# Sixteen small matmuls and a bias row replaced, and convolution taps, weight splits and a square root reordered, in the mixer of a two-block transformer kernel

## The reference, cut to what matters

```
h = layer_norm(x, ln_in_g, ln_in_b)
for l in range(DEPTH):
    proj = h @ w_in[l]
    a_in, b_q, b_k, b_v, c_in, d_cq, d_ckv, d_kr = split(proj)
    a = a_in[..., :256] * sigmoid(a_in[..., 256:])
    a = depthwise_conv(a, conv_a_w[l], conv_a_b[l])          # 31 taps
    o_a = silu(layer_norm(a, ln_a_g[l], ln_a_b[l]))
    o_b = attention(rope(rms(b_q)), rope(rms(b_k)), b_v)     # 4 heads, 2 kv heads
    c = gelu(c_in); u, sv = c[..., :256], c[..., 256:]
    sv = layer_norm(sv, sgu_ln_g[l], sgu_ln_b[l])            # in 4 groups of 64 channels
    sv = einsum('gpq,bnqgc->bnpgc', sgu_w[l], sv) + sgu_b[l].T[:, :, None]
    o_c = u * sv
    o_d = latent_attention(d_cq, d_ckv, d_kr)                # 4 heads, low rank q and k/v
    mix = concatenate([o_a, o_b, o_c, o_d]) @ w_out[l]
    h = layer_norm(ALPHA * h + mix, ...)
    ... feed-forward with a 3-tap convolution, layer_norm
```

## Time and profile before

| | us |
|---|---|
| median of 3 runs | 1983.23 |
| lowest and highest of them | 1982.24, 1985.15 |
| profiled execution, its own time | 1978.52 |
| profiled execution, span of its instructions | 1976.7 |
| PE busy in the span | 1858.6 (94%) |
| DVE busy | 1257.8 (64%) |
| ACT busy | 903.0 (46%) |
| mean granted clock of TensorE | 0.968 |

### The profile page before, as it was taken

One profiled execution on the slowest core, in us unless ns is written; L12 is line 12 of the kernel. 1 busy time (PEld: TensorE's weight loads), 2 busy tenths in 40 slices (PEclk: granted clock), 3 DMA queues, 4 the chain that ended last, 5 costly groups with the idle time before them and its releaser, 6 DMA issues.

```text
span 1976.7 us, 31350 instructions
## 1 busy us (share of the span) xinstructions
PE 1858.6 (94%) x12558; PEld 1683.4 (85%) x12571; DVE 1257.8 (64%) x1550; ACT 903.0 (46%) x1088; POOL 110.2 (6%) x79
## 2 busy tenths in 40 slices
PE   7997699999759999999999999999999998899999
PEld 7975599988549998899898888999899987789998
DVE  5775786787568777655666655555555566546555
ACT  5553454445335444433454555333433357545332
POOL 0300110011002000000016000000000000000000
PEclk9997899999779999999999999999999998999999
DMA  8531265543216554555453362555555542335553
GB/s 296 183 128 52 77 213 191 183 144 113 85 43 222 179 179 145 192 191 181 141 157 120 139 223 87 195 187 191 166 190 186 191 151 86 124 103 166 181 190 127
DMA packets 227044, 311.34 MB, mean 157 GB/s; under 512 B 6615, under 2 KB 199415, under 8 KB 226327
## 3 DMA queue, kind: packets, MB, share of 16 engines
q1 hardware_dynamic: 224038, 298.07, 45.2%
q0 software_dynamic: 2640, 10.66, 1.7%
q10 hardware_dynamic: 288, 1.54, 0.2%
HBM read 307.09 MB, written 3.15 MB: 157 GB/s over the span
## 4 chain that ended last, share of the span: by engine, by line
PE 87%; DVE 5%; ACT 5%; issue 2%; DMA 0%; DVEq 0%; ACTq 0%
PE bank L691 46%; PE bank L947 18%; PE bank L843 7%; PE bank L714 4%; PE bank L700 3%; PE bank L747 1%; ACT w_hi L1556 1%; DVE work L2145 1%; ACT work L1556 1%; DVE w_lo L2148 1%; PE bank L989 1%; PE bank L1100 1%; PE bank L1013 1%; DVE x L2145 1%; PE bank L1140 0%
## 5 line engine op out<-in xcount | busy, mean ns | idle before, releaser
L2148 DVE TENSOR_TENSOR w_lo<-raw,w_hi 128x2048 fp32r<-128x2048 f32 x280 | 642.9, 2304 | 376.1 <-ACT w_hi L1556 375.7
L1556 ACT ACTIVATE w_hi<-raw 128x2048 fp32r<-128x2048 f32 x280 | 532.9, 1904 | 651.5 <-PE bank L691 429.8
L691 PE MATMUL bank<-xt_hi,w_hi 128*128 128x256 f32 x2544 | 723.4, 284 | 4.9 <-DVE w_lo L2148 3.3
L691 PE MATMUL bank<-xt_lo,w_hi 128*128 128x256 f32 x2544 | 721.2, 283 | 0.0
L691 PE MATMUL bank<-xt_hi,w_lo 128*128 128x256 f32 x2544 | 721.1, 283 | 0.0
L691 PEld LDWEIGHTS bank<-xt_hi,w_hi 128*128 128x128 f32 x2544 | 488.7, 192 | 9.3 <-issue 3.7
L691 PEld LDWEIGHTS bank<-xt_lo,w_hi 128*128 128x128 f32 x2544 | 488.9, 192 | 2.3 <-issue 0.2
L691 PEld LDWEIGHTS bank<-xt_hi,w_lo 128*128 128x128 f32 x2544 | 488.9, 192 | 0.0
L947 PE MATMUL bank<-w_hi,act_hi 128*128 128x512 f32 x528 | 206.6, 391 | 0.0
L947 PE MATMUL bank<-w_lo,act_hi 128*128 128x512 f32 x528 | 206.2, 391 | 0.0
L947 PE MATMUL bank<-w_hi,act_lo 128*128 128x512 f32 x528 | 205.4, 389 | 0.0
(11 more groups left out here) (325 smaller groups left out, 2087.7 us busy)
## 6 DMA issues: line engine op xcount, KB each, us to landing
raw<-in_ffn_wi SPq DMA_DIRECT2D x88, 1024.0 KB, 5.1
raw<-in_ffn_w_up SPq DMA_DIRECT2D x44, 1024.0 KB, 5.1
raw<-in_ffn_wo SPq DMA_DIRECT2D x44, 1024.0 KB, 4.8
raw<-in_ffn_w_down SPq DMA_DIRECT2D x22, 1024.0 KB, 5.4
raw<-in_w_in SPq DMA_DIRECT2D x14, 1024.0 KB, 5.3
raw<-in_ssd_in_proj SPq DMA_DIRECT2D x14, 1024.0 KB, 5.2
raw<-in_mem_wkv SPq DMA_DIRECT2D x9, 1024.0 KB, 7.1
raw<-in_w_out SPq DMA_DIRECT2D x8, 1024.0 KB, 4.9
```

What stands on the lines that cost most here:

```text
L691: ins = first(mm(dst, w[s][:, k, c0:c0 + m], xt[v][:, k, :], start=k == 0 and p == 0, stop=k == KT - 1 and p == 2))
L1556: return act.activation(dst, src, ACT.Copy)
L2148: return dve.tensor_tensor(out=out, in0=in0, in1=in1, op=op)
```

## The change

It has four parts, all in `mixer(l)`, and both layers get each of them.

1. **Bias.** `sgu_b` is now spread over the partitions by two small transfers (64 partitions each), the eight one-row matmuls are gone, and `gate_c()` adds the bias on DVE (from PSUM into `g_t`, which frees the bank) before it multiplies with `c_u`. DVE waits there for the transfers (`small_in`).
2. **PE's order.** `branch_c()` stands ahead of `outputs(1)`, `mean_a()` ahead of out-2, and `variance_a()` in the middle of out-2.
3. **ACT's order.** The root for sv stands ahead of `exponentials(1)`; the splits of out-1 and out-3 stand one or more steps earlier (the first ahead of `result(0)`, the last ahead of `turned_pair(2)`).
4. **DVE's order.** The taps are laid out anew (before: one turn after `maxima(1)`, one after `maxima(2)`, one after `maxima(3)`, six at the end; now 1, 2, 1, 2, 1, 2 turns between the other steps), `value_stats()` and `maxima(1)` stand before `finish(0)`, `value_norm()` before `finish(1)`, and the split of out-1 stands behind `operand(1)`, where it stood before `latent_rope()`.

```diff
-        sgu_b = carve("mixer", 4, P, at=0)
+        sgu_b = carve("mixer", 2, P, at=0)
...
-                            mm(dst, c_s[:, n, 64 * g:64 * g + 64], sgu_wt[:, g, :], start=True, stop=False)
-                            ins = mm(dst, cst("ones")[0:1, 0:64], sgu_b[0:1, g, :], start=False, stop=True)
+                            ins = mm(dst, c_s[:, n, 64 * g:64 * g + 64], sgu_wt[:, g, :], start=True, stop=True)
...
                 turn_probs(1)
+                branch_c()
                 outputs(1)
-                branch_c()
...
-                out_rows_of(2)
                 mean_a()
-                variance_a()
+                rows_of = out_unit(units, 2)
+                for tt, h in ORDER:
+                    if (tt, h) == (1, 0):
+                        variance_a()
+                    rows_of(tt, h)
...
                 drained(f"{t}.sw", copy(sgu_wt[:, :, :], b[:, :]))
+                act.wait_ge(var_ready, seen.next(var_ready))
+                act.activation(sd[:, 0:TT], mv[:, :, 1], ACT.Sqrt, bias=eps[:, 0:1]).then_inc(sd_ready, 1)
                 exponentials(1)
...
                 turned_pair(0)
-                act.wait_ge(var_ready, seen.next(var_ready))
-                act.activation(sd[:, 0:TT], mv[:, :, 1], ACT.Sqrt, bias=eps[:, 0:1]).then_inc(sd_ready, 1)
+                split()
                 result(0)
                 turned_pair(1)
                 result(1)
-                split()
                 exponentials(2)
                 split()
                 exponentials(3)
+                split()
                 turned_pair(2)
                 result(2)
                 turned_pair(3)
                 result(3)
-                split()
                 squares_a()
...
-                    drained(f"{t}.c", tt_(mix[:, 4:6, :], two(b[:, :]), c_u[:, :, :], ALU.mult))
+                    dve.wait_ge(small_in, SMALL_AT[t])
+                    drained(f"{t}.c", tt_(g_t[:, :, :].rearrange("p j (n c) -> p j n c", n=TT),
+                                          b[:, :].rearrange("p (j n c) -> p j n c", j=2, n=TT),
+                                          sgu_b[:, :, :].unsqueeze(2).broadcast_to([P, 2, TT, P]), ALU.add))
+                    taken(f"{t}.c")
+                    step(tt_(mix[:, 4:6, :], g_t[:, :, :], c_u[:, :, :], ALU.mult))
...
+                more_taps(13, 1)
                 maxima(0)
-                split()
-                finish(0)
+                more_taps(15, 2)
+                split()
                 value_stats()
                 maxima(1)
-                more_taps(13, 1)
+                finish(0)
                 value_norm()
+                more_taps(19, 1)
                 finish(1)
-                split()
+                more_taps(21, 2)
                 latent_rope()
                 operand(0, "o0", "o1")
                 maxima(2)
-                more_taps(15, 1)
                 gate_c()
                 operand(1, "c")
                 split()
                 finish(2)
+                more_taps(25, 1)
                 maxima(3)
-                more_taps(17, 1)
+                split()
                 finish(3)
+                more_taps(27, 2)
+                dve.memset(st[:, 34:35], 0.0).then_inc(conv_ready, 1)
                 split()
                 operand(2, "o2", "o3")
-                more_taps(19, 6)
-                dve.memset(st[:, 34:35], 0.0).then_inc(conv_ready, 1)
                 center_a()
                 split()
                 scale_a()
...
-                pool.dma_start(sgu_b[0:1, :, :], inp["sgu_b"][l:l + 1]).then_inc(small_in, 16)
+                for i in range(2):
+                    pool.dma_start(sgu_b[64 * i:64 * i + 64, :, :],
+                                   inp["sgu_b"][l, i:4:2, :].partition_broadcast(64)).then_inc(small_in, 16)
```

More of the change, by code:

```diff
@@ L589, in mixed_block_kernel @@
         SMALL_AT, at = {}, 0
-        for phase, n in (("m0", 3), ("m1", 3), ("ssd", 3), ("swa", 3)):
+        for phase, n in (("m0", 4), ("m1", 4), ("ssd", 3), ("swa", 3)):
             at += 16 * n
```

## The result

The changed kernel takes **1925.97 us** (median of 4 runs, 1922.06 to 1928.60), before 1983.24 in the same comparison (1982.24 to 1985.15). The ratio is 0.9709, with a 95% interval of 0.9689 to 0.9728: 57.3 us faster, where the sum forecast 61.8. The profiled execution took 1924.79, with a span of 1923.0 and a mean clock of 0.983 (0.968 before).

What follows compares the result with a forecast made beforehand. PE, busy for 94% of the span, bounds most of the kernel; gains were sought where it waits, each mixer's second half. 11.8 + 3.5 + 0 + 4.2 + 11.4 = 30.9 a layer, twice 61.8, gave 1921.4 us, bounds 1916 to 1939.

Steps and rivals of the forecast that it cites:

- (a): Up to scores(2): it starts at 150.3, set by DVE, instead of 162.08; gain 11.8 us a layer, bounds 10.9 and 13.6.
- (b): scores(2) to out-0: 3.6 us instead of 7.1 at the higher clock, gain 3.5; at the lower clock 1.7.
- (c): out-0 to outputs(3): durations stay, no gain taken; bounds +1.4 and -1.5 us.
- (d): outputs(3) to out-2: only the operand's 1.1 us stands there instead of 5.3; gain 4.2 us a layer.
- (e): out-2 to out-3: 13.1 us instead of 24.5, gain 11.4 a layer; 8 if out-2 ran at the lower clock.
- rival 4: At out-0, the gate waits for the spread bias transfers; could cancel the whole gain if they landed 31 us late; chance 0.02.
- rival 5: Taps find no room because DVE set the pace; (d) and (e) shrink to about 12 a layer, 1960 us; chance 0.04.
- The rule against it: The skill page's drain of about 1.38 us per ACT table switch, 2.66 in all; the forecast took 1.28 per load.
- Rival 3: A table switch on ACT costs 2.7 us; scores(2) starts 2 us later in each layer, 1926; chance 0.05 in full.
- Rival 2: GpSimd is held off by denser DVE work before scores(2); 3.3 us later in each layer, 1928; chance 0.06 in full.
- rival 1: The clock stays low through the middle of the mixer; gain only 23.3 us a layer, 1937; chance 0.13.

Runs made afterwards that it cites:

- no_bias: The changed kernel with the bias part taken back (one-row products again, all new orders kept): 1933.94 us.
- mean_late: The changed kernel with PE's mean and variance of branch a back behind out-2: 1932.85 us.
- taps_mean_late: The changed kernel with mean and variance back behind out-2 and the taps laid nearly as before, DVE's other order kept: 1941.64 us.
- splits_late: The changed kernel with ACT's splits of out-1 and out-3 back behind result(1) and result(3): 1932.40 us.
- bias_only: The kernel before with only the bias part of the change, its PE, ACT and DVE orders as before: 1982.88 us.
- tail_short: The changed kernel with the split of the first feed-forward unit moved behind the activation on ACT and behind operand(3) on DVE: 1909.04 us.

## Why the prediction was right

The terms of the first layer came out as follows (forecast, then measured):

| step | forecast | measured |
|---|---|---|
| (a) `scores(2)` starts | 150.3 (gain 11.8) | 150.30 (162.08 in the earlier trace rows: 11.8) |
| (b) `scores(2)` to out-0 | 3.6 (3.5) | 3.76 (3.4) |
| (c) and (d) out-0 to out-2 | 0 + 4.2 | 26.27 to 20.99 (5.3) |
| (e) out-2 to out-3 | 13.1 (11.4) | 13.28 (11.2) |
| sum of a layer | 30.9 | 31.6 |

- **(a)** The start is right to the tenth partly by luck. The loss beside GpSimd's products was put on `finish(1)`, 3.5; it fell on the four taps ahead of it instead (3.71 for what takes 1.67), and `finish(1)` took its own 1.14. The size was right, 2.04 against 3.30 - 1.14 = 2.2 in the earlier trace rows, the place was not. PE's side was ready at 147.1, not 148.5: `branch_c()` took 0.92, where I had taken 2.2. That had no price, since DVE set the start, but it had one in the bound: without the bias part PE is ready at 151.45 (`no_bias`).
- **(b)** As forecast: maxima, then the gate's first operation at 153.28, then out-0, at a clock of 1.00. The repeated bias tile costs nothing more (0.69), and DVE never waited for the transfers, which rules out rival 4.
- **(c)** Taken as 0 with a bound of +1.4. Out-0 ran at the high clock in the first layer (5.72 for 24 products in the chain view, 7.06 in the earlier trace rows), so the upper bound was nearly the truth there.
- **(d)** Out-2 starts 1.29 after `result(3)` (173.37 + 0.39 to 175.05), 1.1 forecast. The last tap is done at 169.8, 5 us before out-2, so rival 5 is out too.
- **(e)** The split between variance and out-3 stays, as forecast. `mean_late` (20.3) and `taps_mean_late` (24.1) show that mean and taps each hold a part of this gain. The splits belong to (d): in `splits_late` out-2 starts at 180.52, behind 4.67 of idle time on PE where after has 0.72.
- **The rule against it.** The root ends and the second load begins with no gap (133.66 + 0.29, then 133.98), and the exponentials start at 135.27, 1.29 after it. The Trainium skill, page "ScalarE: Activation LUTs", section "What ACT_TABLE_LOAD costs", adds a drain of about 1.38 to each switch; the switch at 141.07 in the earlier trace rows and the two above show none. Rival 3 is out.
- **Rival 2** is out by the GpSimd rows: its operations went through at 136.57 and 138.02, 1.37 and 1.34 each, and it was DVE that gave way. The Trainium skill, page "SBUF — State Buffer", section "SBUF: two separate sides", says that the one that starts first holds the shared port for its whole instruction and the other blocks; DVE's loss of 2.04 beside 2.71 of GpSimd work agrees with it in the main: one after the other, taps and GpSimd's work would have taken 1.67 + 2.71 = 4.38, and the taps were done in 3.71.
- **Two slips in the working** changed nothing. The upper bound of a layer is 34.1 by its own terms (13.6 + 3.5 + 1.4 + 4.2 + 11.4), not 33.6. And PE didn't stand through the 10.04 of 24 taps: it did out-2 beside the first 7.44 of them, and waited 2.55 for the last, the 2.5 of rival 5.

**What was over-estimated is the factor of two.** The sum is right for a layer in which `scores(2)` and out-0 have the higher clock; in the second layer `scores(2)` ran at 0.50, and out-0 behind it at 0.72. `scores(2)` to out-0 took 5.39 for 3.76, and out-0 to `scores(3)` 7.54 for 5.6 (154.06 to 159.6): 3.6 given back. That is rival 1's mechanism, in one layer and two steps, and the runs give it a better chance than my 0.13: of the five traces with the same wait of 3.20 ahead of `scores(2)`, all show a clock below 1.00 in `scores(2)` or in out-0 behind it, in one layer or both. `splits_late` is the mildest: `scores(2)` took 1.97 in both layers, but out-0 to `scores(3)` took 7.2 in the first (a clock of 0.76) and 5.5 in the second.

By the marks, after is 30.8 ahead of before behind the first mixer (31.6 less 0.8, since out-3 and the norm took 15.11, 14.27 before, with more of out-3 at the lower clock), 58.1 behind the second, 57.3 at the second block, and 53.8 behind the state-space stretch, in which after pays the 3.5 and before didn't. That is the 53.7 between the two profiled executions.

The medians differ by 57.3, since the profiled execution of before lay 4.7 below its median and that of after 1.2. The four runs of after order themselves by their clock: 0.985 at 1922.06, 0.983 at 1924.79, 0.982 at 1927.15, 0.981 at 1928.60. The 4.7 of before are mostly the state-space stretch: the profiled `bias_only`, which keeps pace with before up to there (984.1 and 983.8) and pays the 3.5, took 1982.40, near the median of before. Of the 29 executions of before beside the experiments two came below 1979, at 1978.51 and 1978.67, both with the mean clock of the profiled one, 0.968; the other 27 have 0.965 or 0.966. So the medians most likely compare executions that both pay it, and their 57.3 is the 57.3 of the third mark; that step is argued, since those executions weren't traced.

## What to carry to other kernels

Look in a windows view for stretches in which PE is half idle, and read the clock beside it: taking a wait away there also speeds up what runs behind it, so the price of a wait can be more than its length (here `tail_short` took 4.0 out of a wait and got 6.0 in that stretch). A part can be worth nothing alone and 8 us with the others, when two engines were late by turns; undo parts from the finished kernel to see their worth, don't only add them to the old one. When one layer repeats another, look at the clock in each before doubling. And before reading a few microseconds out of two single traces, compare stretches of equal work far from the change: here one of them moves 3.5 by itself.

## What the runs showed of the hardware

- **The clock fell in a stretch in which PE was busy throughout.** In the state-space mixer of after, in windows of 4 us of the same kernel:

```profile
966.00:970.00 4.00, 4.00 (x21) 4.00 (x20) 3.64 (x7) 0.47 (x2) 0.00 (x0) 0.50 0.42 119
970.00:974.00 4.00, 4.00 (x20) 4.00 (x21) 1.21 (x6) 3.03 (x5) 0.00 (x0) 0.50 0.42 146
...
926.49:1043.47 116.98, 115.41 (x842) 109.41 (x843) 77.65 (x115) 58.50 (x70) 33.89 (x30) 0.94 0.38 118
```

The last row is the state-space mixer proper. In before the same 842 products took 113.49:

```profile
983.82:1097.31 113.49, 112.14 (x842) 106.23 (x843) 76.40 (x115) 58.21 (x70) 40.24 (x30) 0.97 0.39 122
```

PE was busy for the whole of the 38 us between the start of the stretch and the fall in after, so no idle time there explains it, and the change doesn't touch this part. The clock fell in before too, at the same place in the stretch (0.69 in the 4 us from 1023.84), but for less long: an estimate from the clock of windows of 4 us gives some 3 us at the lower level, against some 10 in after. Of the twelve traces eight pay the 3.5, as the table of marks shows by rows like this one (of after; first and last start):

```profile
L714 PE MATMUL bank<-xt_hi,w_hi x32: 278/283/415, 926.5 to 1106.7; 128*128 128x256 f32 x32
```

What decides it is open: no kernel here tried it. `bias_only` and before have the same program in this stretch and start it at 984.1 and 983.8, and only `bias_only` pays. A second such place is in `no_bias`: the clock fell in `outputs(1)` with PE busy for 7.42 of 7.42 us (0.91 in the mean), behind the alternating one-row products.

- **The same wait, the same program, another clock.** `scores(2)` behind a wait of 3.20 took 1.97 in after and 2.77 in `tail_short` in the first layer, where the two have the same program up to there, and 3.75 and 1.97 in the second.
- **A one-row product behind each full one costs more than its rows.** At the high clock, 0.18 for each array instruction when they alternate (`no_bias`) and 0.058 when only full ones follow each other (after); at the low one 0.31 (before) and 0.12 (`bias_only`). Why they are slower in alternation was not tried.
- **GpSimd took from DVE most of its own time.** Four taps with two operands in SBUF took 3.71 beside 2.71 of GpSimd work, in place of 1.67: 2.04 lost. In before `finish(1)` lost 2.2 beside two operations of 1.26. GpSimd's operations took 1.37 and 1.34, 0.1 more than the 1.26 of the earlier trace rows.
